# Expert rows added into two rows of DRAM for each token, in place of eight rows written once

## The chip, the cores and the metric

One core of a Trainium2 chip runs the whole kernel in one launch. The metric is the device time of the kernel in microseconds (us). The kernel before takes 988.71 us, the median of three runs (987.71 to 989.04).

## What is computed

One layer of a decoder on 512 tokens of width 1024, in float32. After the mixers and attention comes a mixture of experts, and it is the part that the change touches:

```python
idx, wts = route(h2, w_router[i], router_bias[i])            # 8 of 64 experts for each token
y = swiglu(h_pad[tok], w_gate[e], w_up[e], w_down[e])        # for each expert e, its tokens tok
acc = acc.at[tok].add(y.astype(jnp.float32) * wt[:, None])   # weighted rows, summed for each token
x = x + moe.reshape(B, S, D)                                 # moe: this sum plus a shared expert
ple_gate = jax.nn.sigmoid(rmsnorm(x, g_ple[i]) @ w_ple_gate[i])
x = x + ple_gate * rmsnorm(p[i] @ w_ple_proj[i], g_ple_post[i])
```

So 512 x 8 = 4096 weighted rows of 4 KB each have to be brought together by token. Each expert has three weight matrices of 1 MB, 192 MB in all.

## The kernel before, in words

**Stages.** The dense part (attention, mixers, gates) ends at about 300 us. Then the router, the lists of tokens and the shared expert, then the experts from about 343 us to about 904 us, and then a tail: the sum of the routed rows, and the per-layer gate `w_ple_gate` on the four tiles of 128 tokens.

**The expert loop.** The experts are sorted by the number of their tokens and taken four at a time, in 16 groups. A group is three steps of 128 slots in the first eight groups (96 slots for each expert) and two steps in the others (64 slots each), 40 steps (`STEPS`). No step holds slots of more than two experts. In a step r:

- GpSimd (POOL) gathers 128 token rows from DRAM by an indirect DMA (`gather`, L791), four steps before it handles the output rows of the same step.
- TensorE transposes the rows (L1740), multiplies by the gate and up matrices (`up`, L2196), transposes the activations (L2205) and multiplies by the down matrix (`down(r)`, L2225, one iteration later).
- ScalarE scales the 128 output rows by their weights (`weigh`, L971) into one of two buffers `yrow`.
- GpSimd sends them to DRAM by an indirect DMA (`scatter`, L801 to L810) into `y_dram`, named accumulator in the trace, at row 8 x token + rank, where rank says which of its eight experts this is for the token. Slots with no token have an index out of bounds and move nothing. `scatter(r)` waits for the landing of scatter r-2, which used the same buffer.

SyncE (SP) issues the weight loads in an order written out by hand (`load_group`): each waits until TensorE has finished with its slot of the buffer `ring` (`gu_ps` counts the gate and up products, `y_ps` the down products). After the experts it issues the `w_ple_gate` loads (`load_ple_gate`, L616), which need slots 9, 10, 0 and 11.

**The lists.** Once for all tokens, VectorE (DVE) turns the sorted ranks into a running count over the experts (L1491 to L1499), which becomes the fourth column of `tokw`, beside three bfloat16 parts of the weight. For each group TensorE picks weight and rank of each slot by small matmuls (`lists`), and `weights_of` (L1504 to L1536) turns them into scale and index with seven small VectorE instructions.

**The last group.** Its rows for the first tile of tokens are not scattered; TensorE adds them by `picked_rows` (L2268), and VectorE by `add_picked` (L1617). For this, and for that only, the eight rows of each token of tile 0 were set to zero early on (L502, 4096 KB).

**The tail.** The tokens are cut into ten `PIECES`: four of 256 columns for tile 0, and two of 512 columns for each other tile. `load_rows` (L463) reads eight part rows for each token into the ring: 16 MB in 20 DMAs. `sum_eight` (L1622 to L1624) adds eight to four to two to one, `sum_rows` (L1692) adds the total to x and counts `x2_ready`. TensorE then transposes (`third_T`, L2324), VectorE scales the transposed columns (L1698), and TensorE multiplies by `w_ple_gate` (`ple_gate_part`, L2340). ScalarE takes the sigmoid (L1042), VectorE forms the result (L1711, L1713), SP stores it. Piece 0 is loaded by ScalarE's queue and pieces 1 to 3 by SP before the last scatter has landed, those of tiles 1 to 3 after `experts_done` (set at L847 when all scatters have landed), and the later ones also wait for a buffer: five buffers serve ten pieces (`Y_FREED`).

There is also a path for lists longer than 96 (`further_rounds`); it is not taken with these inputs.

Of the kernel before, what the change touches and what calls it, by code (L numbers as in the profile page):

```python
# [14 lines left out]
P = 128  # L15
# [19 lines left out]
ACC_ROWS = T * TOPK  # L35
# [19 lines left out]
TCOL, WCOL = 2, 4  # L55
# [112 lines left out]
Y_FREED = [0, 0, 0, 0, 0, 1, 3, 4, 5, 6]  # L168
# [11 lines left out]
def build(nc, t, y_dram, h2_dram, out):  # L180
    ctx = ExitStack()
    with ctx:
# [3 lines left out]
        def sem(name):  # L186
# [61 lines left out]
        slot_wr = qa[:, 1024 + 3 * STEPS:1024 + 5 * STEPS].rearrange("p (r c) -> p r c", c=2)  # L248
# [20 lines left out]
        count_of = flat_actT[:, 2 * D:2 * D + 3 * NR].rearrange("p (b i e) -> p b i e", b=2, i=NT)  # L269
# [6 lines left out]
                 for k in range(2)]  # L276
# [6 lines left out]
        pair_sum, pair_own = (small[:, 40 + k * 12:52 + k * 12].rearrange("p (s e c) -> p s e c", e=2, c=2)  # L283
                              for k in range(2))
        ysum = [ring[:, s:s + n // 256, :].rearrange("p u n -> p (u n)").rearrange("p (r n) -> p r n", r=TOPK)
                for s, (_, _, n) in zip(Y_SLOT, PIECES)]

# [63 lines left out]
        y_loaded = [sem(f"y_loaded{b}") for b in range(5)]  # L351
# [82 lines left out]
        y_rows = y_dram.rearrange("(i p r) n -> i p r n", p=P, r=TOPK)  # L434
# [39 lines left out]
        def _(sp):  # L474
# [27 lines left out]
            sp.dma_start(y_rows[0], zero_row.unsqueeze(1).broadcast_to([P, TOPK, D])).then_inc(y_first, 16)  # L502
# [127 lines left out]
            for m in range(2, 4):  # L630
                for c in range(2):
                    load_rows(sp, m, c)

            def o_start(j):
                sp.wait_ge(y_ps, STRIPS * STEPS)
                for b in range(4):
                    sp.wait_ge(y_loaded[b], 32)
# [8 lines left out]
            def o_reload():  # L646
                sp.wait_ge(o_done, 1)
                for m in range(4):
                    for c in range(2):
                        load_rows(sp, m, c, y_first)  # L650
# [16 lines left out]
        def _(pool):  # L667
# [157 lines left out]
            def o_move(e, n, j):  # L825
# [11 lines left out]
                                        yrow[0][0:CAP, :], None, bounds_check=ACC_ROWS - 1, oob_is_err=False  # L837
                                        ).then_inc(o_scattered, 16)
# [21 lines left out]
        def _(act):  # L860
# [104 lines left out]
            def weigh(r):  # L965
                j = r % BUF
                act.wait_ge(y_ps, STRIPS * (r + 1))
                act.wait_ge(list_ready, STEP_OF[r][0] + 1)
                if r >= BUF:
                    act.wait_ge(scattered[j], 16 * (r // BUF))  # L970
                nc.scalar.activation(yrow[j], bank(6, 2), ACT.Copy, scale=slot_wr[:, r, 0:1]).then_inc(y_ready, 1)  # L971
# [21 lines left out]
            for r in range(STEPS):  # L993
# [7 lines left out]
                if r == STEPS - 1:  # L1001
                    for j in range(BUF):
                        act.wait_ge(scattered[j], 16 * len(range(j, STEPS - DIRECT, BUF)))
                    for c in range(2):
                        load_rows(act, 0, c)
# [50 lines left out]
        def _(dve):  # L1056
# [391 lines left out]
            HEAD, SMALL = NE // 2, BIG_GROUPS * GROUP  # L1448
# [38 lines left out]
            nc.vector.tensor_copy(tw3[:, :, 2], rest)  # L1487
# [11 lines left out]
            nc.vector.tensor_scalar(tokw[:, :, :, 3], count_of[:, b, :, HEAD:], -1.0, None, ALU.add  # L1499
                                    ).then_inc(tokw_ready, 1)  # L1500
# [3 lines left out]
            def weights_of(g, found):  # L1504
# [5 lines left out]
                own = cst[:, C_PAIR:C_PAIR + 6] if g < BIG_GROUPS else cst[:, C_PAIR2:C_PAIR2 + 4]  # L1510
                total = pair_sum[:, 0:n, :, :]
                mine = pair_own[:, 0:n, :, :]
                nc.vector.tensor_copy(total[:, :, :, 1], w[:, :, :, 3]).then_inc(dve_step, 1)
                nc.vector.tensor_copy(mine[:, :, :, 0], w[:, :, :, 0]).then_inc(dve_step, 1)
                n_step[0] += 2
                dve.wait_ge(dve_step, n_step[0])
                link(nc.vector.tensor_tensor(total[:, :, :, 0], mine[:, :, :, 0], w[:, :, :, 1], ALU.add))
                link(nc.vector.tensor_tensor(total[:, :, :, 0], total[:, :, :, 0], w[:, :, :, 2], ALU.add))
                link(nc.vector.tensor_tensor(
                    mine, total, own.rearrange("p (s e) -> p s e", e=2).unsqueeze(3).broadcast_to([P, n, 2, 2]),  # L1520
                    ALU.mult))
                link(nc.vector.tensor_tensor(slot_wr[:, r, :], mine[:, :, 0, :], mine[:, :, 1, :], ALU.add))
                rank_of = slot_wr[:, r, 1]
                if g == NGROUP - 1:


                    first, rank_of = small[:, 16:16 + n], small[:, 20:20 + n]
                    link(nc.vector.tensor_scalar(first, row_of[:, r], float(P), float(ACC_ROWS), ALU.is_lt, ALU.mult))
                    link(nc.vector.tensor_tensor(rank_of, first, slot_wr[:, r, 1], ALU.add))
                nc.vector.scalar_tensor_tensor(to_row[:, r], row_of[:, r], float(TOPK), rank_of,  # L1530
# [108 lines left out]
            def o_vector(e, n, j):  # L1639
# [7 lines left out]
                def o_link(ins):  # L1647
# [13 lines left out]
                nc.vector.scalar_tensor_tensor(o_to[0:CAP, :], row, float(TOPK), L[:, 5:6], ALU.mult, ALU.add  # L1661
                                               ).then_inc(o_list_ready, 1)
# [10 lines left out]
            def o_rows():  # L1673
                dve.wait_ge(y_first, 16 * 9)
                nc.vector.tensor_reduce(first_sum, ysum[0].rearrange("p r n -> p n r"), AX_X, ALU.add
                                        ).then_inc(y_first, 1)
                dve.wait_ge(y_first, 16 * 9 + 1)
# [4 lines left out]
            def sum_rows(m):  # L1682
# [3 lines left out]
                total = ysum[m][:, 0, :] if m else first_sum  # L1686
                if m:
                    dve.wait_ge(y_loaded[Y_BUF[m]], 32 * (1 + Y_BUF[0:m].count(Y_BUF[m])))
                    sum_eight(m, total)
# [693 lines left out]
```

## Time and profile before

| | |
|---|---|
| median of 3 runs | 988.71 us (987.71 to 989.04) |
| the profiled execution | 985.47 us |
| span of its profile | 983.6 us |
| mean granted TensorE clock | 0.989 |
| busy: PE, DVE, ACT, POOL | 930.8, 360.6, 162.6, 229.8 us |
| moved by DMA | 298.95 MB |

The profile is of one execution; a sum of its rows is made against its span of 983.6 us, and 985.47 us is that execution's own time, with 1.9 us around the span. Busy time of PE counts overlapping matmuls; shares of DMA are those of the core's 16 DMA engines.

### The profile page before, as it was taken

What the parts mean: (1) busy time and instruction counts of PE and PEld (TensorE: products, weight loads), DVE (VectorE), ACT (ScalarE), POOL (GpSimd) and SP (SyncE); (2) the same over time, 40 slices, a digit from 0 to 9 for tenths busy, and PEclk for the clock granted to TensorE, in tenths of its full rate; (3) what the DMA queues carried; (4) which work ended last, traced back from release to release, by engine and by line L of the source; (5) the groups of instructions that cost most, each with busy time, mean ns of one, the idle gap of its engine ahead of it and who ended that gap; (6) DMA issues with size and microseconds to landing.
All of it is one profiled execution on the core that took longest, in us unless ns stands there. A gap on an engine that the chain in (4) does not pass through costs nothing.

```text
span 983.6 us, 15583 instructions
## 1 busy us (share of the span) xinstructions
PE 930.8 (95%) x6327; PEld 477.3 (49%) x6327; DVE 360.6 (37%) x773; ACT 162.6 (17%) x304; POOL 229.8 (23%) x345
## 2 busy tenths in 40 slices
PE   6999999999999999999999999999879898997698
PEld 4678788888655533333333333333323333332345
DVE  5565673336436743333332111111101111111787
ACT  2001324210011211111111111111101111221021
POOL 4115923162110212222222222211211111101110
PEclk9999999999999999999999999999979999999899
DMA  9930005421393659999999999999999999999972
GB/s 331 332 129 1 1 1 175 167 86 51 131 382 154 214 209 397 398 416 403 406 418 409 409 420 413 419 420 422 412 422 423 419 422 411 420 404 365 379 279 86
DMA packets 81816, 298.95 MB, mean 304 GB/s; under 512 B 9251, under 2 KB 33863, under 8 KB 57552
## 3 DMA queue, kind: packets, MB, share of 16 engines
q1 hardware_dynamic: 68048, 261.09, 67.2%
q0 software_dynamic: 11920, 33.63, 8.7%
q10 hardware_dynamic: 1776, 3.21, 0.9%
q8 instruction: 51, 0.84, 0.3%
q14 instruction: 21, 0.17, 0.1%
HBM read 277.16 MB, written 29.36 MB: 312 GB/s over the span
## 4 chain that ended last, share of the span: by engine, by line
PE 74%; DMA 20%; SPq 3%; DVE 2%; issue 1%; ACT 1%; POOL 0%; POOLq 0%; ACTq 0%
PE ps L2196 23%; DMA ring<-in_w_exp_up 16%; PE ps L1807 12%; PE ps L2225 9%; PE ps L1957 6%; PE ps L1936 5%; PE ps L2340 4%; PE ps L1763 3%; PE ps L1740 2%; SPq L463 2%; PE ps L2012 1%; PE ps L1769 1%; DMA ring<-accumulator 1%; PE ps L2205 1%; DMA accumulator<-actT,stage 1%; SPq L517 1%
## 5 line engine op out<-in xcount | busy, mean ns | idle before, releaser
L2196 PE MATMUL ps<-ring,gates 128*32 128x512 f32 x2560 | 287.7, 601 | 25.4 <-DMA ring<-in_w_exp_up 24.7
L2196 PEld LDWEIGHTS ps<-ring,gates 128*32 128x32 f32 x2560 | 88.0, 111 | 217.3 <-issue 216.4
L2225 PE MATMUL ps<-ring,poolbuf 128*32 128x512 f32 x1280 | 145.6, 595 | 3.1 <-DMA ring<-in_w_exp_down 3.1
L1554 DVE COPY poolbuf<-ps 128x256 f32<-128x256 f32 x40 | 17.0, 425 | 352.7 <-PE ps L2205 352.7
L2225 PEld LDWEIGHTS ps<-ring,poolbuf 128*32 128x32 f32 x1280 | 37.9, 109 | 83.9 <-issue 82.2
L784 POOL COPY stage<-qT 128x1 uint32<-128x1 uint32 x40 | 7.2, 180 | 261.1 <-PE ps L1740 233.4
L971 ACT ACTIVATE actT<-ps,qT 128x1024 f32<-128x1024 f32 x40 | 44.5, 1113 | 142.3 <-PE ps L2225 142.3
L963 ACT ACTIVATE poolbuf<-ps 128x256 f32<-128x256 f32 x40 | 15.3, 384 | 277.5 <-PE ps L2196 277.5
L1807 PE MATMUL ps<-xrow,ring 128*128 128x256 f32 x256 | 57.9, 381 | 0.1
L1957 PE MATMUL ps<-ring,gates 128*128 128x512 f32 x128 | 56.4, 594 | 0.0
L1740 PE MATMUL ps<-cst,rows 128*128 128x128 f32 x352 | 48.5, 285 | 7.8 <-DVE rows L1067 7.7
L773 POOL TENSOR_TENSOR tickets<-cst 128x1 f32<-128x1 f32 x78 | 14.6, 188 | 163.2 <-ACT actT L971 159.8
L1807 PEld LDWEIGHTS ps<-xrow,ring 128*128 128x128 f32 x256 | 48.4, 190 | 8.4 <-issue 1.7
L1740 PEld LDWEIGHTS ps<-cst,rows 128*128 128x128 f32 x352 | 44.7, 193 | 9.9 <-issue 8.5
L1807 PE MATMUL ps<-actT,ring 128*128 128x256 f32 x208 | 47.5, 382 | 0.0
L791 POOL DMA_INDIRECT rows<-h_rows,stage x40 | 42.0, 1050 | 21.0 <-issue 18.8
L808 POOL DMA_INDIRECT accumulator<-actT,stage x40 | 40.6, 1015 | 22.0 <-issue 22.0
L2340 PE MATMUL ps<-ring,actT 128*128 128x512 f32 (+1 forms) x112 | 42.2, 531 | 0.0
L1807 PEld LDWEIGHTS ps<-actT,ring 128*128 128x128 f32 x208 | 39.1, 190 | 6.3 <-issue 0.9
L723 POOL TENSOR_TENSOR ring<-ring 128x1024 f32<-128x1024 f32 x12 | 28.3, 2358 | 52.7 <-DMA ring<-in_w_gate 30.5
L1957 PEld LDWEIGHTS ps<-ring,gates 128*128 128x128 f32 x128 | 23.8, 190 | 26.8 <-issue 26.8
L691 POOL TENSOR_SCALAR st<-st 128x1 f32<-128x1 f32 (+2 forms) x17 | 4.3, 255 | 110.5 <-ACT rows L916 49.7
(288 smaller groups left out, 1069.6 us busy)
## 6 DMA issues: line engine op xcount, KB each, us to landing
ring<-in_w_exp_down SPq DMA_DIRECT2D x64, 1024.0 KB, 17.3
ring<-in_w_exp_gate SPq DMA_DIRECT2D x62, 1024.0 KB, 14.0
ring<-in_w_exp_up SPq DMA_DIRECT2D x62, 1024.0 KB, 15.7
ring<-accumulator SPq DMA_DIRECT2D x12, 1024.0 KB, 13.0
ring<-in_w_gate SPq DMA_DIRECT2D x8, 1024.0 KB, 10.3
ring<-in_w_in SPq DMA_DIRECT2D x5, 1024.0 KB, 12.9
xrow<-in_x SPq DMA_DIRECT2D x8, 512.0 KB, 5.2
accumulator<-ring SPq DMA_DIRECT2D x1, 4096.0 KB, 19.8
```

The source lines that it names most:

```text
L723: nc.gpsimd.tensor_tensor(dst, a, b, ALU.subtract).then_inc(wsum_ready, 1)
L791: pool.indirect_dma_start(hg[j], None, h2_dram, bass.IndirectOffsetOnAxis(ap=stage[:, 0, j, :], axis=0), bounds_check=T - 1, oob_is_err=Fa ...
L808: pool.indirect_dma_start(y_dram, bass.IndirectOffsetOnAxis(ap=stage[:, 1, j, :], axis=0), yrow[j], None, bounds_check=ACC_ROWS - 1, oob_i ...
L971: nc.scalar.activation(yrow[j], bank(6, 2), ACT.Copy, scale=slot_wr[:, r, 0:1]).then_inc(y_ready, 1)
L1740: last = nc.tensor.transpose(bank(b0 + half)[:, k * width:(k + 1) * width], v[0:width, 4 * half + k, :], ident[0:width, 0:width])
L1763: last = mm(bank(2 * (i % 2)), actT[:, k, i * P:(i + 1) * P], qv[:, k], start=(k == 0), stop=(k == KD - 1))
L1807: last = mm(out[:, f * HALF_T:(f + 1) * HALF_T], w[:, k, f * P:(f + 1) * P], x[:, k, :], start=(k == 0), stop=(k == 3))
L1936: last = mm(bank(2 + c % 4)[:, f * HALF_T:(f + 1) * HALF_T], w[:, k, (2 * p + f) * P:(2 * p + f + 1) * P], x[:, k, :], start=(k == 0), sto ...
L1957: last = mm(bank(half), gates[:, k, i * P:(i + 1) * P], w[:, k], start=(n == 0), stop=(n == KD - 1))
L2196: last = mm(bank(2 + k)[part, :], hgT[k][:, q, part], pair_view(EXPERT_SLOT[js[c]])[:, q], start=(q == 0), stop=(q == KD - 1))
L2225: last = mm(bank(6 + half)[part, :], eactT[r % 2][:, q, part], w[:, q, half * 512:(half + 1) * 512], start=(q == 0), stop=(q == 1))
L2340: last = mm(gate_bank(i, n0)[:, 0:width], xT, unit_view(s, 4)[:, k % 4, n0 % 512:n0 % 512 + width], start=(k == 0), stop=(k == KD - 1))
```

## The change

The accumulator shrinks from eight rows for each token to two. A scatter now adds to a row (`compute_op=ALU.add`) in place of writing it. The row is 2 x token + part, where part is 0 or 1 by which of the step's two experts the slot belongs to, so that no DMA names a row twice; since successive DMAs may name the same row, each scatter waits for the landing of the one before it. The 1024 rows are set to zero early by one DMA of 4096 KB, as large as before. The running count, the rank column and part of `weights_of` go. At the end each tile is read by one DMA of 1 MB, tile 0 by ScalarE's queue and the others by SP after `experts_done`; each tile has a ring slot of its own. One addition takes the place of `sum_eight`.

```diff
-ACC_ROWS = T * TOPK
+PARTS = 2
+ACC_ROWS = T * PARTS
...
-Y_SLOT = [1, 3, 4, 7, 5, 1, 3, 7, 5, 1]
-Y_BUF = [0, 1, 2, 3, 4, 0, 1, 3, 4, 0]
+Y_SLOT = [1, 3, 4, 7]
...
-        def load_rows(eng, m, c, done=None):
-            i, c0, width = PIECES[m]
-            eng.dma_start(ysum[m][:, 4 * c:4 * c + 4, :], y_rows[i][:, 4 * c:4 * c + 4, c0:c0 + width]
-                          ).then_inc(y_loaded[Y_BUF[m]] if done is None else done, 16)
+        def load_rows(eng, i, done=None):
+            eng.dma_start(ring[:, Y_SLOT[i], :], y_rows[i]).then_inc(y_loaded[i] if done is None else done, 16)
...
-            sp.dma_start(y_rows[0], zero_row.unsqueeze(1).broadcast_to([P, TOPK, D])).then_inc(y_first, 16)
+            sp.dma_start(y_all, zero_row.unsqueeze(1).broadcast_to([P, ACC_ROWS // P, D])).then_inc(y_first, 16)
...
             load_ple_gate(0, 0)
             load_ple_gate(0, 1)
-            for j in range(BUF):
-                sp.wait_ge(scattered[j], 16 * len(range(j, STEPS - DIRECT, BUF)))
-            sp.wait_ge(gu_ps, STRIPS * STEPS)
-            for c in range(2):
-                load_rows(sp, 1, c)
             load_ple_gate(1, 0)
             sp.wait_ge(y_ps, STRIPS * (STEPS - 1))
             load_ple_gate(1, 1)
-            for m in range(2, 4):
-                for c in range(2):
-                    load_rows(sp, m, c)
...
             sp.wait_ge(experts_done, 1)
-            for m in range(4, NPIECE):
-                if Y_FREED[m]:
-                    sp.wait_ge(x2_ready, Y_FREED[m])
-                load_rows(sp, m, 0)
-                load_rows(sp, m, 1)
+            for i in range(1, NT):
+                load_rows(sp, i)
...
             def scatter(r):
                 j = r % BUF
-                if r >= BUF:
-                    pool.wait_ge(scattered[j], 16 * (r // BUF))
+                if r:
+                    pool.wait_ge(scattered[(r - 1) % BUF], 16 * ((r - 1) // BUF + 1))
...
                 pool.indirect_dma_start(y_dram, bass.IndirectOffsetOnAxis(ap=stage[:, 1, j, :], axis=0),
-                                        yrow[j], None, bounds_check=ACC_ROWS - 1, oob_is_err=False
-                                        ).then_inc(scattered[j], 16)
+                                        yrow[j], None, bounds_check=ACC_ROWS - 1, oob_is_err=False,
+                                        compute_op=ALU.add).then_inc(scattered[j], 16)
...
-                    for c in range(2):
-                        load_rows(act, 0, c)
+                    load_rows(act, 0)
...
-            dve.wait_ge(shared_ps, 2)
-            for b in range(2):
-                nc.vector.memset(count_of[:, b, :, 0:HEAD], 0.0).then_inc(dve_step, 1)
-            n_step[0] += 2
-            link(nc.vector.tensor_scalar(count_of[:, 0, :, HEAD:], rank3, 0.5, None, ALU.is_gt))
-            b, span = 0, 1
-            while span < NE:
-                link(nc.vector.tensor_tensor(count_of[:, 1 - b, :, HEAD:], count_of[:, b, :, HEAD:],
-                                             count_of[:, b, :, HEAD - span:HEAD - span + NE], ALU.add))
-                b, span = 1 - b, 2 * span
...
                 link(nc.vector.tensor_tensor(
-                    mine, total, own.rearrange("p (s e) -> p s e", e=2).unsqueeze(3).broadcast_to([P, n, 2, 2]),
-                    ALU.mult))
-                link(nc.vector.tensor_tensor(slot_wr[:, r, :], mine[:, :, 0, :], mine[:, :, 1, :], ALU.add))
-                rank_of = slot_wr[:, r, 1]
+                    mine, w, own.unsqueeze(3).broadcast_to([P, n, 2, WCOL]), ALU.mult))
+                link(nc.vector.tensor_reduce(slot_w[:, r], mine.rearrange("p s e c -> p s (e c)"), AX_X, ALU.add))
+                part = own[:, :, 1]
...
-            def sum_eight(m, total):
-                y = ysum[m]
-                link(nc.vector.tensor_tensor(y[:, 0:4, :], y[:, 0:4, :], y[:, 4:8, :], ALU.add))
-                link(nc.vector.tensor_tensor(y[:, 0:2, :], y[:, 0:2, :], y[:, 2:4, :], ALU.add))
-                link(nc.vector.tensor_tensor(total, y[:, 0, :], y[:, 1, :], ALU.add))
-            dve.wait_ge(y_loaded[Y_BUF[0]], 32)
-            sum_eight(0, first_sum)
+            def sum_parts(m, total):
+                i, c0, width = PIECES[m]
+                y = ysum[i][:, :, c0:c0 + width]
+                return nc.vector.tensor_tensor(total, y[:, 0, :], y[:, 1, :], ALU.add)
+            dve.wait_ge(y_loaded[0], 16)
+            link(sum_parts(0, first_sum))
```

## Rows read from the trace of the kernel before

**Rows 1.** The page: engine totals, and the span in 40 equal slices.

```profile
PE 930.8 (95%) x6327; PEld 477.3 (49%) x6327; DVE 360.6 (37%) x773; ACT 162.6 (17%) x304; POOL 229.8 (23%) x345
...
PE   6999999999999999999999999999879898997698
...
DMA  9930005421393659999999999999999999999972
GB/s 331 332 129 1 1 1 175 167 86 51 131 382 154 214 209 397 398 416 403 406 418 409 409 420 413 419 420 422 412 422 423 419 422 411 420 404 365 379 279 86
```

**Rows 2.** The page: DMA queues (packets, MB, share of 16 engines' span).

```profile
q1 hardware_dynamic: 68048, 261.09, 67.2%
q0 software_dynamic: 11920, 33.63, 8.7%
```

**Rows 3.** Windows: span, busy of PE, PEld, DVE, ACT, POOL, clock, DMA share, GB/s.

```profile
345.00:380.00 35.00, 34.27 (x360) 13.71 (x355) 13.83 (x46) 5.17 (x8) 6.90 (x15) 1.00 0.70 265
380.00:571.00 191.00, 191.00 (x1920) 73.90 (x1916) 56.88 (x206) 32.39 (x47) 46.93 (x95) 1.00 1.00 409
571.00:630.00 59.00, 58.82 (x534) 21.25 (x526) 6.77 (x15) 10.47 (x15) 14.08 (x30) 1.00 1.01 417
630.00:903.00 273.00, 245.41 (x1850) 90.69 (x1842) 37.67 (x73) 40.47 (x66) 42.07 (x90) 0.97 1.01 415
```

**Rows 4.** Chain that ended last, in order of time (start, length, what): expert stage.

```profile
547.66 6.87 PE ps L2196 x64
...
559.42 6.98 PE ps L2196 x64
...
578.87 15.97 DMA ring<-in_w_exp_up
...
848.10 24.19 DMA ring<-in_w_exp_up
```

**Rows 5.** Timeline of POOL (start, length), one of the 40 steps.

```profile
453.15 1.01 POOL L808 DMA_INDIRECT accumulator<-actT,stage  x1 [0.55 <-issue]
...
460.26 1.04 POOL L791 DMA_INDIRECT rows<-h_rows,stage  x1 [0.50 <-issue]
461.31 0.58 POOL L801 COPY stage<-qT 128x1 uint32<-128x1 uint32 x1
464.55 0.19 POOL L773 TENSOR_TENSOR tickets<-cst 128x1 f32<-128x1 f32 x1 [2.66 <-ACT actT L971]
465.29 1.02 POOL L808 DMA_INDIRECT accumulator<-actT,stage  x1 [0.55 <-issue]
```

**Rows 6.** Chain that ended last: from the last scatters to the end.

```profile
886.53 8.49 DMA accumulator<-actT,stage
...
916.93 11.35 DMA ring<-accumulator
...
940.37 6.87 PE ps L2340 x16
947.23 0.44 PE ps L2324 x4
...
969.61 10.36 PE ps L2340 x40
```

**Rows 7.** Timeline of 868 to 935 us, all engines.

```profile
899.93 3.64 PE L2225 MATMUL ps<-ring,poolbuf 128*32 128x512 f32 x32 [1.02 <-DMA ring<-in_w_exp_down]
...
900.59 0.99 POOL L808 DMA_INDIRECT accumulator<-actT,stage  x1 [0.52 <-issue]
...
903.50 3.70 PE L2268 MATMUL ps<-actT,poolbuf 128*128 128x512 f32 x8
...
905.69 0.99 POOL L808 DMA_INDIRECT accumulator<-actT,stage  x1 [0.53 <-issue]
...
910.95 1.28 DVE L1617 TENSOR_TENSOR xrow<-xrow,ps 128x512 f32<-128x512 f32 x2
912.27 0.43 DVE L1692 TENSOR_TENSOR xrow<-xrow,gates 128x256 f32<-128x256 f32 x1
...
913.25 0.09 POOL L847 MEMSET tickets<- 128x1 f32 x1 [6.56 <-DMA accumulator<-actT,stage]
```

**Rows 8.** Timeline of 335 to 352 us: the running count and what lies beside it.

```profile
343.08 7.07 PE L2196 MATMUL ps<-ring,gates 128*32 128x512 f32 x64
...
344.44 2.73 DVE L1496 TENSOR_TENSOR actT<-actT 128x256 f32<-128x256 f32 x6
```

**Rows 9.** DMA issues: engine, count, KB each, median us to landing.

```profile
ring<-in_w_branch_b SPq DMA_DIRECT2D x2, 1024.0 KB, 5.2
```

More of the change, by code:

```diff
@@ L54 @@
 FIRST_STEP = [STEP_OF.index((g, 0)) for g in range(NGROUP)]
-TCOL, WCOL = 2, 4
+TCOL, WCOL = 2, 3
 LCOL = TCOL + 2 * WCOL
@@ L282, in build @@
         zero_row = ring[:, 10, 0:D]
[L283 to L286, printed above, removed]
+        pair_own = small[:, 40:40 + 3 * 2 * WCOL].rearrange("p (s e c) -> p s e c", e=2, c=WCOL)
+        ysum = [ring[:, s, :].rearrange("p (r n) -> p r n", r=PARTS) for s in Y_SLOT]
         ps = ctx.enter_context(nc.psum_tensor("ps", [P, 8 * 512], F32))
@@ L350, in build @@
         y_first, o_done = sem("y_first"), sem("o_done")
-        y_loaded = [sem(f"y_loaded{b}") for b in range(5)]
+        y_loaded = [sem(f"y_loaded{i}") for i in range(NT)]
         in_first_loaded = sem("in_first_loaded")
@@ L629, in _ @@
             load_ple_gate(1, 1)
-            for m in range(2, 4):
-                for c in range(2):
-                    load_rows(sp, m, c)
             def o_start(j):
                 sp.wait_ge(y_ps, STRIPS * STEPS)
-                for b in range(4):
-                    sp.wait_ge(y_loaded[b], 32)
+                sp.wait_ge(y_loaded[0], 16)
             def o_load(e, n, j):
@@ L647, in o_reload @@
                 sp.wait_ge(o_done, 1)
-                for m in range(4):
-                    for c in range(2):
-                        load_rows(sp, m, c, y_first)
+                load_rows(sp, 0, y_first)
             further_rounds(sp, longest_list(sp), o_start, o_load, o_reload)
@@ L836, in o_move @@
                 pool.indirect_dma_start(y_dram, bass.IndirectOffsetOnAxis(ap=o_to[0:CAP, :], axis=0),
-                                        yrow[0][0:CAP, :], None, bounds_check=ACC_ROWS - 1, oob_is_err=False
-                                        ).then_inc(o_scattered, 16)
+                                        yrow[0][0:CAP, :], None, bounds_check=ACC_ROWS - 1, oob_is_err=False,
+                                        compute_op=ALU.add).then_inc(o_scattered, 16)
                 pool.wait_ge(o_scattered, 16 * (n + 1))
@@ L970, in weigh @@
                     act.wait_ge(scattered[j], 16 * (r // BUF))
-                nc.scalar.activation(yrow[j], bank(6, 2), ACT.Copy, scale=slot_wr[:, r, 0:1]).then_inc(y_ready, 1)
+                nc.scalar.activation(yrow[j], bank(6, 2), ACT.Copy, scale=slot_w[:, r:r + 1]).then_inc(y_ready, 1)
             def ple_square(n):
@@ L1003, in _ @@
                         act.wait_ge(scattered[j], 16 * len(range(j, STEPS - DIRECT, BUF)))
-                    for c in range(2):
-                        load_rows(act, 0, c)
+                    load_rows(act, 0)
                 if r:
@@ L1486, in _ @@
             link(nc.vector.tensor_tensor(rest, rest, tw3[:, :, 1], ALU.subtract))
[L1487 to L1500 removed]
+            nc.vector.tensor_copy(tw3[:, :, 2], rest).then_inc(tokw_ready, 1)
             shared_mult(1)
@@ L1509, in weights_of @@
                 w = found[:, :, TCOL:].rearrange("p s (e c) -> p s e c", e=2)
-                own = cst[:, C_PAIR:C_PAIR + 6] if g < BIG_GROUPS else cst[:, C_PAIR2:C_PAIR2 + 4]
-                total = pair_sum[:, 0:n, :, :]
+                own = (cst[:, C_PAIR:C_PAIR + 6] if g < BIG_GROUPS else cst[:, C_PAIR2:C_PAIR2 + 4]).rearrange(
+                    "p (s e) -> p s e", e=2)
                 mine = pair_own[:, 0:n, :, :]
[L1513 to L1518, printed above, removed]
                 link(nc.vector.tensor_tensor(
-                    mine, total, own.rearrange("p (s e) -> p s e", e=2).unsqueeze(3).broadcast_to([P, n, 2, 2]),
-                    ALU.mult))
-                link(nc.vector.tensor_tensor(slot_wr[:, r, :], mine[:, :, 0, :], mine[:, :, 1, :], ALU.add))
-                rank_of = slot_wr[:, r, 1]
+                    mine, w, own.unsqueeze(3).broadcast_to([P, n, 2, WCOL]), ALU.mult))
+                link(nc.vector.tensor_reduce(slot_w[:, r], mine.rearrange("p s e c -> p s (e c)"), AX_X, ALU.add))
+                part = own[:, :, 1]
                 if g == NGROUP - 1:
-                    first, rank_of = small[:, 16:16 + n], small[:, 20:20 + n]
+                    first, part = small[:, 16:16 + n], small[:, 20:20 + n]
                     link(nc.vector.tensor_scalar(first, row_of[:, r], float(P), float(ACC_ROWS), ALU.is_lt, ALU.mult))
-                    link(nc.vector.tensor_tensor(rank_of, first, slot_wr[:, r, 1], ALU.add))
-                nc.vector.scalar_tensor_tensor(to_row[:, r], row_of[:, r], float(TOPK), rank_of,
+                    link(nc.vector.tensor_tensor(part, first, own[:, :, 1], ALU.add))
+                nc.vector.scalar_tensor_tensor(to_row[:, r], row_of[:, r], float(PARTS), part,
                                                ALU.mult, ALU.add).then_inc(list_ready, 1)
@@ L1660, in o_vector @@
                 nc.vector.tensor_copy(o_from[0:CAP, :], row)
-                nc.vector.scalar_tensor_tensor(o_to[0:CAP, :], row, float(TOPK), L[:, 5:6], ALU.mult, ALU.add
-                                               ).then_inc(o_list_ready, 1)
+                nc.vector.tensor_tensor(o_to[0:CAP, :], row, row, ALU.add).then_inc(o_list_ready, 1)
                 dve.wait_ge(o_hgT_ps, 2 * n + 1)
@@ L1673, in o_rows @@
             def o_rows():
[L1674 to L1677, printed above, removed]
+                dve.wait_ge(y_first, 32)
+                sum_parts(0, first_sum).then_inc(y_first, 1)
+                dve.wait_ge(y_first, 33)
             further_rounds(dve, longest, o_start, o_vector, o_rows)
@@ L1685, in sum_rows @@
                 xs = xrow[:, i, c0:c0 + width]
-                total = ysum[m][:, 0, :] if m else first_sum
+                total = ysum[i][:, 0, c0:c0 + width] if m else first_sum
                 if m:
-                    dve.wait_ge(y_loaded[Y_BUF[m]], 32 * (1 + Y_BUF[0:m].count(Y_BUF[m])))
-                    sum_eight(m, total)
+                    dve.wait_ge(y_loaded[i], 16)
+                    link(sum_parts(m, total))
                 else:
```

9 lines of the change are left out of this document (4 added, 5 removed).

## The prediction

> **What bounds the kernel now.** I read the page first. PE is busy 95% of the span, but the slices show that in the expert stage, from the 16th slice on, the DMA engines are at nine tenths or more too, and that PE has eights and sevens there towards the end while DMA has none until the last two slices [rows 1]. So two resources compete for the title and the share of busy time can't decide it. The windows say which: from 380 to 571 us PE never idles while DMA moves 409 GB/s, and from 571 us on DMA moves 415 to 417 GB/s and PE has gaps, 27.6 us of them from 630 to 903 us alone [rows 3]. The chain of waits agrees: up to 571 us it is PE after PE, a step of 12.1 to 12.2 us each, with a first DMA wait at 578.87 us, and after that it runs along the weight loads [rows 4]. The expert stage is therefore bound by the bytes that the 16 DMA engines move, in its first part by a hair less than PE.
>
> The tail I read from the chain and the timeline together. The last down product starts at 899.93 and ends at 903.57 us. The first x2 piece is ready at 912.70 (912.27 + 0.43), and the chain then runs along the accumulator reads until about 928 us and from 940 us on along PE alone [rows 6, 7]. So the tail has a part that is bound by reading 16 MB and a part that is bound by PE, and I must see how long PE alone would need.
>
> **The price of adding in the scatter.** The software queue moved 33.63 MB in 40 gathers and 40 scatters, so one scatter carries about 0.42 MB (80 DMAs, the same rows in and out). The queues' shares per MB are the same, 0.257% for q1 and 0.259% for q0 [rows 2]: a byte costs the engines the same whoever sends it. Now the accumulating DMA has to read the destination row besides the source row. No row of this trace shows such a DMA, so I bound it. Let e be the extra engine time of a scatter as a multiple of what it takes now. Below, e = 0: the second read hides in the engine. Above, e = 2: read, read and write follow one another where a plain one overlaps read and write. I take e = 1, the nearest row's price per byte applied to a second read of the same length.
>
> The scatters that come while DMA is full and before the last weight lands are r = 1 to 37: the 38th scatter is issued at 886.53, the next at 900.59, after the last weight wait of PE at 899.93 [rows 6, 7]; the first is before 380 us, where the share is 0.70 [rows 3]. That is 37 x 0.42 = 15.5 MB. At 420 GB/s, what the full slices show [rows 1], e = 1 costs 37 us. There is a little room: from 380 to 571 us, 191 x 409/420 = 186, so 5 us of idle engine time take the first of it. **The expert stage grows by 32 us** (e = 0: 0; e = 2: 69).
>
> No run before this one shows a second read's cost; the Trainium skill, "Collectives: The Full Stack", section on the bandwidth ceiling, says that an add in the DMA engine is slowed not by the arithmetic but by two source reads on one ring, at a measured ratio of 1.93 for its ring reduction. By that e would be 0.93 and the growth 29 us, an estimate from that page.
>
> **The new wait.** Scatter r now waits for scatter r-1 before POOL copies its indices. Behind it on POOL stand the ticket, the scatter itself and the next gather. In steady state a scatter is issued at 453.15, the next index copy stands at 461.31, and the next ticket at 464.55, when ScalarE's rows are there [rows 5]. A scatter under full DMA load landed in 8.49 us [rows 6]. So from 453.15 on there are 11.4 us until the rows are ready, and a landing up to 11 us costs nothing. A longer one delays scatters at first without harm, since the buffers `yrow` are needed two steps later and a gather has some two steps of lead. It binds only if landing plus copy, ticket and issue (0.2 + 0.2 + 0.55, about 1.3 us with semaphores) exceeds the step, which will be some 12.8 us when DMA sets it (12.15 x 409/420, and 1.0 us for 0.42 MB at 420 GB/s). From 8.5 us I expect 10 to 11. Priced at nothing in the loop.
>
> **The tail.** What PE has to do from the first x2 piece on: for each tile two halves of 6.87 and 0.44 us [rows 6], 14.6 us, 58.5 us for four tiles (the last one's quarter-width pieces add up to the same). It takes from 912.70 to 969.61 + 10.36 = 979.97, 67.3 us. So 8.8 us are idle for want of rows or for the addition, and these go. The start moves too: tile 0's two rows come in 1 MB instead of 4 MB, before the last products end; then the first x2 piece waits only for the picked rows, 903.50 + 3.70, plus 1.28 and 0.43 [rows 7]: 908.9 instead of 912.7, another 3.8. Together 12.5 us. Against it stands the serial landing of the last two scatters. They are issued at 900.59 and 905.69 now [rows 7]. With the wait the last can't go before 900.6 + 10 + 1.3 = 912, and lands at some 920 (the last one took 7.6 us to the mark at 913.25 [rows 7]); tile 1 is then loaded in about 5 us (a 1 MB load in a quiet stretch landed in 5.2 [rows 9]), added and transposed in 2.5 us: 928. PE is through with tile 0 at 908.9 + 1.2 + 14.6 = 924.7. So 3 us come back. **The tail shrinks by 9 us**, and the reading of 12 MB less is worth no more than that, since PE is what is left.
>
> **The rest, at nothing.** The running count is ten VectorE instructions, six of them 2.73 us together, so at most 4.6 us at that price each, beside TensorE's first products of 7.07 us [rows 8]; its first reader comes at step 1, 12 us later. Without that cover they would be a gain of up to 4.6 us. Four fewer small instructions for each group, two columns fewer in the list matmuls and two additions less for each piece lie on engines that wait for TensorE or DMA in this stage. The zeros are 4096 KB before and after. The `w_ple_gate` loads stand behind every expert weight in SP's queue still, and come earlier than before by the removed waits; they are in time for tile 0 either way.
>
> **Sum.** +32 - 9 = +23 on the profiled span: 983.6 to 1006.6. The profiled execution took 985.47, 3.2 below the median of 988.71; on the median the sum is 1011.7, call it 1012.
>
> **Rivals.** (a) The second read is free or nearly so, e below 0.3. For it: the shares [rows 2] are of packets and not of either direction, so they can't exclude it. Against it: DMA is full, and a read of HBM is what it is full of. The stage grows by 0 to 6 us, the tail gives 9 to 12: 977 to 986, faster. It decides where e falls under about 0.38, where 37e - 5 = 9. (b) e between 0.3 and 0.7: 986 to 1001. (c) Read, read and write don't overlap, or the rows are added with a stall in the engine: e from 1.4 to 2.2, stage +47 to +76, 1027 to 1056. (d) The scatters' own chain becomes the bound: with a landing of 14 us a step of the first eight groups takes 15.3 in place of 12.2, 24 x 3.1 = 74, and the other 16 steps, at 17 us bound by DMA, still take 1 us more each: +90 - 9, 1070. It speaks for it that 8.5 us is already two thirds of a step; against it, that only the engines' part of this landing doubles (6.4 rows of 4 KB for each engine, 1 us at 420/16 GB/s, 2 us when shared with the loads).
>
> **How the numbers follow.** Forecast (e from 0.7 to 1.4) 0.55; (a) 0.13, (b) 0.07, (c) 0.16, (d) 0.09. The time is that of the likeliest, 1012, whose own range is 1001 to 1027. The range for eight in ten leaves out the lower half of (a) and (d) and the end of (c): 983 to 1052. About 0.2%, 2 us, is what a measurement of this kernel can tell from no change. Faster by more than that holds (a) and nothing else, 0.13; within it is the foot of (b), 0.03; slower is the rest, 0.84.
>
> **What would show it.** Right, if in the profile after: the software queue's share of the engines grows by about half of 8.7% or more for the same rows; the steps before 571 us take about 12.8 us in place of 12.15, with DMA and not PE at their head in the chain; the last down product starts near 932 instead of 899.9; POOL's wait for the scatter before shows only small sums; and from the first x2 piece to the end of PE it is about 62 us in place of 67. Wrong, if the last down product stays near 900 (a), if it comes after 950 (c), or if POOL's index copy waits for the landing in every step and PE for ScalarE's or POOL's rows (d). A tail that shrinks by more than 15 us would mean that I missed a wait there.

## The result, and the profile after

The kernel after takes 1022.18 us (median of four runs, 1021.26 to 1023.43) where the kernel before takes 988.21 us (four runs): a ratio of 1.0339 with a 95% interval of 1.0321 to 1.0357, 34 us more. 1012 us was forecast, with a range of 983 to 1052. The direction and the mechanism were right, two terms of the size were not: the expert stage, to the start of the last down product, grew by 47.5 us in place of 32, and the tail shrank by 11.7 in place of 9.

First the page of the profile after: totals, the 40 slices and the queues.

```profile
span 1019.4 us, 15473 instructions
...
PE 943.0 (93%) x6327; PEld 480.5 (47%) x6327; DVE 319.5 (31%) x679; ACT 162.9 (16%) x304; POOL 250.0 (25%) x345
...
DMA  9830005322665489999999999999999999999612
GB/s 331 309 124 1 1 17 191 124 83 83 259 247 227 166 317 390 382 385 358 367 392 344 366 389 349 380 390 402 376 399 396 387 404 386 389 400 353 218 72 83
...
q1 hardware_dynamic: 58976, 248.51, 61.6%
q0 software_dynamic: 11920, 33.64, 12.7%
```

The software queue moves the same 33.6 MB as before [rows 2], but holds the engines for 12.7% of 1019.4 = 129.5 us in place of 8.7% of 983.6 = 85.6. The 43.9 us more are just over the 42.8 that 40 scatters took before (half of 85.6), so e is 1.03 by this view, if the gathers still take their half. The MB listed don't include the second reads; the share does. The same kernel without the add (`e1_plain`, below) lists the same MB at the old share:

```profile
q0 software_dynamic: 11920, 33.63, 8.8%
```

This is why GB/s falls below 400 while DMA stays at nine.

The windows of the same stretches (as in [rows 3]: span, busy of PE, PEld, DVE, ACT, POOL, clock, DMA share, GB/s) show the stage going over to the DMA bound from its first third on:

```profile
380.00:571.00 191.00, 180.03 (x1770) 68.72 (x1763) 47.07 (x148) 29.45 (x43) 48.72 (x85) 0.96 1.00 375
571.00:630.00 59.00, 51.28 (x438) 18.82 (x440) 6.41 (x15) 8.79 (x14) 13.65 (x25) 0.94 0.98 362
630.00:903.00 273.00, 240.33 (x1790) 88.23 (x1786) 35.32 (x68) 38.12 (x61) 54.82 (x96) 0.95 1.01 392
```

Before 571 us PE never waited; now it idles 11 us there, and its granted clock is 0.96 in place of 1.00. The timeline of PE shows how: five waits for gate and up weights up to 630 us, some 40 us apart, of which the three longest are followed by slower products (start, length, and in brackets the idle time and what ended it).

```profile
455.16 9.61 PE L2153 MATMUL ps<-ring,gates 128*32 128x512 f32 x64 [4.50 <-DMA ring<-in_w_exp_up]
...
469.87 7.05 PE L2153 MATMUL ps<-ring,gates 128*32 128x512 f32 x64
...
495.63 7.07 PE L2153 MATMUL ps<-ring,gates 128*32 128x512 f32 x64 [1.31 <-DMA ring<-in_w_exp_up]
537.41 9.44 PE L2153 MATMUL ps<-ring,gates 128*32 128x512 f32 x64 [5.16 <-DMA ring<-in_w_exp_up]
577.39 7.07 PE L2153 MATMUL ps<-ring,gates 128*32 128x512 f32 x64 [1.74 <-DMA ring<-in_w_exp_up]
618.84 9.69 PE L2153 MATMUL ps<-ring,gates 128*32 128x512 f32 x64 [5.98 <-DMA ring<-in_w_exp_up]
```

The slower products run in part at half of the full clock, as this window shows (columns as above, clock 0.50):

```profile
455.10:457.50 2.40, 2.34 (x12) 0.69 (x16) 0.00 (x0) 0.00 (x0) 0.00 (x0) 0.50 1.02 432
```

The waits add up to 18.7 us and the extra length of the three products to 7.6 (9.61 + 9.44 + 9.69 - 3 x 7.05). Scatter 20 is issued at 635.59 us in place of 609.12: 26.5 us later, which is about their sum.

The new wait, in the timeline of POOL one step of the 40, to be read beside [rows 5]:

```profile
440.70 1.61 POOL L789 DMA_INDIRECT accumulator<-actT,stage  x1 [0.55 <-issue]
...
447.81 1.07 POOL L772 DMA_INDIRECT rows<-h_rows,stage  x1 [0.50 <-issue]
451.05 0.18 POOL L782 COPY stage<-qT 128x1 uint32<-128x1 uint32 x1 [2.17 <-DMA accumulator<-actT,stage]
452.10 0.19 POOL L754 TENSOR_TENSOR tickets<-cst 128x1 f32<-128x1 f32 x1 [0.87 <-ACT actT L952]
```

The index copy waits 2.17 us for the scatter before, which landed 10.3 us after its issue, and then POOL still waits 0.87 us for ScalarE's rows. Over the kernel the landings are these (the view of the scatter's line):

```profile
DMA to landing us min/median/max: 4.5/10.5/11.9
```

The tail in the timeline: the last down product, the picked rows, the first x2 piece, the last scatter and the reads.

```profile
947.38 3.64 PE L2182 MATMUL ps<-ring,poolbuf 128*32 128x512 f32 x32 [1.04 <-DMA ring<-in_w_exp_down]
...
950.95 3.70 PE L2225 MATMUL ps<-actT,poolbuf 128*128 128x512 f32 x8
...
953.93 1.45 DVE L1577 TENSOR_TENSOR xrow<-xrow,ps 128x512 f32<-128x512 f32 x2 [5.41 <-PE ps L2225]
955.41 0.42 DVE L1649 TENSOR_TENSOR xrow<-xrow,gates 128x256 f32<-128x256 f32 x1
...
958.90 1.57 POOL L789 DMA_INDIRECT accumulator<-actT,stage  x1 [1.27 <-issue]
```

And its end in the chain that ended last:

```profile
958.90 4.45 DMA accumulator<-actT,stage
...
963.66 4.76 DMA ring<-accumulator
968.42 0.02 issue
968.45 0.70 DVE ring L1583
...
1005.39 10.36 PE ps L2297 x40
```

This chain goes back no further than 957.17 us, so what stands at the head of the early steps is read from the timeline of PE above. From the start of the last down product to the end of the span it is 72.0 us (1019.4 - 947.38); before it was 83.7 [rows 7]. From the first x2 piece, ready at 955.83 (955.41 + 0.42), to the end of PE at 1015.75 it is 59.9 us in place of 67.3.

### The profile page after: what moved, and what is told of

The parts are those of the page before. It is cut to its first block and busy times, and to the rows that moved or that the text cites. A ratio compares the mean times of both kernels' runs of the same rounds, so it can differ in the third digit from the quotient of the medians.

```text
span 1019.4 us, 15473 instructions
## 1 busy us (share of the span) xinstructions
PE 943.0 (93%) x6327; PEld 480.5 (47%) x6327; DVE 319.5 (31%) x679; ACT 162.9 (16%) x304; POOL 250.0 (25%) x345
## 3 DMA queue, kind: packets, MB, share of 16 engines
q0 software_dynamic: 11920, 33.64, 12.7%
## 5 line engine op out<-in xcount | busy, mean ns | idle before, releaser
L2153 PE MATMUL ps<-ring,gates 128*32 128x512 f32 x2560 | 300.2, 623 | 56.5 <-DMA ring<-in_w_exp_up 55.7
L2153 PEld LDWEIGHTS ps<-ring,gates 128*32 128x32 f32 x2560 | 91.3, 114 | 258.5 <-issue 257.6
L789 POOL DMA_INDIRECT accumulator<-actT,stage x40 | 64.2, 1605 | 23.0 <-issue 23.0
L1764 PE MATMUL ps<-actT,ring 128*128 128x256 f32 x208 | 47.5, 381 | 0.0
L1914 PEld LDWEIGHTS ps<-ring,gates 128*128 128x128 f32 x128 | 23.8, 190 | 26.8 <-issue 26.8
## 6 DMA issues: line engine op xcount, KB each, us to landing
ring<-in_w_gate SPq DMA_DIRECT2D x8, 1024.0 KB, 11.7
ring<-in_w_in SPq DMA_DIRECT2D x5, 1024.0 KB, 12.7
```

Of the source, the lines that this page charges most:

```text
L1764: last = mm(out[:, f * HALF_T:(f + 1) * HALF_T], w[:, k, f * P:(f + 1) * P], x[:, k, :], start=(k == 0), stop=(k == 3))
L1914: last = mm(bank(half), gates[:, k, i * P:(i + 1) * P], w[:, k], start=(n == 0), stop=(n == KD - 1))
L2153: last = mm(bank(2 + k)[part, :], hgT[k][:, q, part], pair_view(EXPERT_SLOT[js[c]])[:, q], start=(q == 0), stop=(q == KD - 1))
```

## The experiments

Times are medians beside runs of the kernel before on the same chip (987.5 to 988.3 us in each set); intervals are of the ratio to it.

**Is it the add or the wait?** Three kernels take the change apart. The first takes the add out of the kernel after:

```diff
-                                        yrow[j], None, bounds_check=ACC_ROWS - 1, oob_is_err=False,
-                                        compute_op=ALU.add).then_inc(scattered[j], 16)
+                                        yrow[j], None, bounds_check=ACC_ROWS - 1, oob_is_err=False
+                                        ).then_inc(scattered[j], 16)
```

> The kernel after with a plain writing scatter in place of the adding one; two rows for each token, the wait for the scatter before and the short tail stay (so most expert rows are overwritten and the output lacks them). Theory A (the second read of the adding DMA fills the engines): the expert stage falls back to its old length, the tail stays 11.6 us shorter, about 977 us. Theory B (the wait for the scatter before costs a good part of the 47 us): at least 990 us. Theory C (the tail's gain depends on the shift): not near either.

Measured: 976.09 us, 0.9884 (0.9867 to 0.9900), 11.6 us under the kernel before, and 46.1 under the kernel after. The new wait, with plain scatters, costs about nothing: the last down product starts 1.2 us later than before:

```profile
901.08 3.64 PE L2182 MATMUL ps<-ring,poolbuf 128*32 128x512 f32 x32 [1.79 <-DMA ring<-in_w_exp_down]
```

The tail is 73.3 us long. So nearly the whole growth of the stage goes with the add, and 10.4 us of the tail's gain are there without it.

The second takes the wait away by giving even and odd steps an accumulator each:

```diff
-                if r:
-                    pool.wait_ge(scattered[(r - 1) % BUF], 16 * ((r - 1) // BUF + 1))
+                if r >= BUF:
+                    pool.wait_ge(scattered[j], 16 * (r // BUF))
...
-                pool.indirect_dma_start(y_dram, bass.IndirectOffsetOnAxis(ap=stage[:, 1, j, :], axis=0),
+                pool.indirect_dma_start(y_odd if r % 2 else y_dram,
+                                        bass.IndirectOffsetOnAxis(ap=stage[:, 1, j, :], axis=0),
```

> The kernel after with two accumulators, one for even and one for odd steps, so that a scatter waits for the one before the last only; the tail reads the even one alone (the output lacks the odd steps' rows). The odd one is zeroed by a 4 MB copy while DMA is idle early on. Theory A: same as after, 1020 to 1024 us. Theory B: 1012 us or less.

Measured: 1022.66 us, 1.0360 (1.0343 to 1.0377), as the kernel after. Adds without the wait cost the same.

The third puts the add into the kernel before, into its eight rows, all of which are set to zero early:

```diff
+            for i in range(1, NT):
+                eng.dma_start(y_all[i], y_all[0]).then_inc(y_zeroed, 16)
...
-                                        yrow[j], None, bounds_check=ACC_ROWS - 1, oob_is_err=False
-                                        ).then_inc(scattered[j], 16)
+                                        yrow[j], None, bounds_check=ACC_ROWS - 1, oob_is_err=False,
+                                        compute_op=ALU.add).then_inc(scattered[j], 16)
```

> The kernel before with an adding scatter into its eight rows, all zeroed early while DMA is idle; no new wait, the old tail. Theory A: the expert stage grows by 47 us as in after and the tail keeps its length: 1033 to 1037 us. Theory B (wait): much less of the 47 us, under 1020 us.

Measured: 1034.93 us, 1.0485 (1.0468 to 1.0503): 47.2 us more, with the old wait and the old tail. 47.2 - 11.6 = 35.6 is the change's 34 within the runs' spread. Theory B, the wait, has fallen: the growth is there in both kernels that add without it, and the wait without the add costs 1.2 us.

**Is it the bytes?** The kernel before gets a second transfer behind each scatter. First a plain copy, then half of it:

```diff
+                pool.dma_start(spare[r], h2_dram[0:P, 0:820]).then_inc(y_zeroed, 16)
```

> The kernel before with one plain DMA of 0.42 MB from DRAM to DRAM issued by GpSimd behind each scatter: the same bytes as the second reads, without an add. Theory A (bytes and nothing else): the same growth as the eight-row add, 1033 to 1037 us. Theory D (an add holds the engines longer than its bytes): 10 us or more less, 1025 us at most.

Measured: 1025.93 us, 1.0401 (1.0382 to 1.0420), 38.2 us more; the last down product starts 38.1 us later than before:

```profile
937.99 5.06 PE L2228 MATMUL ps<-ring,poolbuf 128*32 128x512 f32 x32 [2.40 <-DMA ring<-in_w_exp_down]
```

So 0.42 MB cost 0.96 us each over 40 copies, near the 1.0 us of the prediction's price by bytes, but the add costs 9 us more than this. Theory A had 1033 to 1037 us and is missed by 7; theory D had at most 1025 and is missed by 1, so that at this point D stood the better.

> The kernel before with a plain copy of 0.21 MB behind each scatter, half of the extra copy of 0.42 MB that cost 38 us. If bytes cost in proportion, 19 us: 1007 us. If the first 5 us of engine time are free, as the prediction had it, the full copy's 38 was 43 less 5 and the half is 16.5: 1004 us or less.

Measured: 1008.08 us, 1.0211 (1.0193 to 1.0230), 19.7 us more, about half of 38.2. There are no free first 5 us.

Then the same rows a second time, as a plain scatter:

```diff
+                pool.indirect_dma_start(spare, bass.IndirectOffsetOnAxis(ap=stage[:, 1, j, :], axis=0),
+                                        yrow[j], None, bounds_check=ACC_ROWS - 1, oob_is_err=False
+                                        ).then_inc(scattered[j], 16)
```

All waits for a scatter count both.

> The kernel before with every scatter sent twice, as a plain write, the second time into a spare array at the same rows: the same source, the same 4 KB rows, the same 0.42 MB as the second read of an adding scatter. If the adding DMA holds the engines longer than a plain transfer of the same rows, the growth is that of the plain copy, 37 to 40 us: 1025 to 1028 us. If the plain copy was cheap because of its shape (3.3 KB rows, DRAM to DRAM) and rows of a scatter simply cost more, the growth is that of the add, 46 to 49 us: 1034 to 1037 us.

Measured: 1034.38 us, 1.0472 (1.0455 to 1.0490), 46.9 us more, and the last down product where the kernel after has it:

```profile
947.39 3.64 PE L2228 MATMUL ps<-ring,poolbuf 128*32 128x512 f32 x32 [1.24 <-DMA ring<-in_w_exp_down]
```

So the theory that an add holds the engines longer than a plain transfer (D) has fallen too. An adding scatter costs what two plain scatters of the same rows cost; it is rows of these lists that cost a fifth more than the same bytes in an even copy (46.9 against 38.2 us). The copy differs from a scatter in three things, the even spread, the source in DRAM and the rows of 3.3 KB, and this run doesn't tell which of them counts.

**Where in the stage?** The add in one half of the steps only, in the kernel after:

```diff
-                                        compute_op=ALU.add).then_inc(scattered[j], 16)
+                                        **({"compute_op": ALU.add} if r < 20 else {})).then_inc(scattered[j], 16)
```

> The kernel after with the add in the scatters of steps 0 to 19 only, plain writes in the others (so rows are overwritten). Theory A1 (the price is 1.0 to 1.1 us for each adding scatter wherever it stands): 20 us on top of 976, 996 us. Theory A2 (in the first eight groups, where TensorE and DMA are nearly even, an add costs more, because each DMA wait of TensorE is followed by products at half clock): 26 us on top, 1000 to 1004 us. The 5 us of room of the prediction: 991 us.

> The kernel after with the add in the scatters of steps 20 to 39 only, plain writes in the others. Theory A1: 18 to 20 us on top of 976, 994 to 996 us. Theory A2: the same or a little less than A1, 992 to 995 us, and the two halves together give the whole growth of 47 us.

Measured: 1002.60 us, 1.0147 (1.0132 to 1.0163), and 997.63 us, 1.0098 (1.0081 to 1.0114). Against 976.09 without adds that is 26.5 and 21.5 us, 48 together. The second run is the same with `r >= 20`. Theory A1, one price everywhere, missed by 6.6 us on the first half and 1.6 on the second; A2 named the first, but had the second 2.6 us too low.

**Why do listed rows cost more?** A list is cut into strips of 32 slots and fills them from the front; the empty slots move nothing. If a DMA engine serves fixed partitions, the ones that serve the front of a strip carry more rows. Of the 128 slots each engine would have 8. Counted over the lists of this input, with four neighbouring partitions in each 32 of its half of the partitions for an engine, the fullest carries 311 of the 4096 rows and the mean is 256, a factor of 1.21; the double scatter cost 1.23 times the even copy. The Trainium skill, "DMA: Bandwidth & Descriptors", section on the descriptor swizzle, gives that assignment of partitions to engines, for a full 1 MB transfer; no view here shows which engine carries which rows. The test spreads the slots, by one table:

```diff
+    c[:, C_SLOT + 1:C_SLOT + CAP + 1] = slot // STRIP * STRIP + slot % 4 * 8 + slot % STRIP // 4 + 1
...
-                        cst[:, C_IOTA + low:C_IOTA + CAP + 1].unsqueeze(1).unsqueeze(1).broadcast_to(
+                        cst[:, C_SLOT + low:C_SLOT + CAP + 1].unsqueeze(1).unsqueeze(1).broadcast_to(
```

> The kernel before, with one table of constants changed: inside each strip of 32 slots the r-th row of a list goes to slot 4 x (r mod 8) + r div 8 in place of slot r, so that the filled slots of a partly filled strip are spread over the partitions. Same rows, same bytes, same output. Theory E (a list that fills its strips from the front loads some of the 16 DMA engines with more rows than others, and the stage goes by the fullest one: over all steps 311 rows for it against a mean of 256, by counting the lists if each engine serves four neighbouring partitions in each 32 of its half; spread it has 270): gathers and scatters get cheaper, and where DMA sets the pace, from about 571 us on, that shows: 977 to 984 us. If engines don't differ: 987 to 989 us.

Measured: 981.75 us, 0.9941 (0.9928 to 0.9955), 5.8 us less.

> The kernel after with the same table. Theory E: the adding scatter moves three shares of rows in place of two through the fullest engine, so the gain is larger than in the kernel before, 41 rows x 3 x 0.156 us = 19 us at most, nearly all of it where DMA sets the pace: 1003 to 1008 us. If engines don't differ: 1021 to 1023 us.

Measured: 1005.08 us, 1.0180 (1.0160 to 1.0199), 17.1 us less than the kernel after. The windows of this kernel:

```profile
380.00:571.00 191.00, 182.57 (x1826) 71.00 (x1822) 48.41 (x151) 31.41 (x45) 51.85 (x91) 0.99 1.02 389
571.00:630.00 59.00, 58.30 (x530) 21.21 (x525) 6.76 (x15) 9.61 (x15) 15.25 (x28) 1.00 1.02 388
```

The rate listed is 389 GB/s in place of 375, for the same rows and bytes, and PE's clock is back at 0.99 in this stretch. The same permutation gains three times as much where each list passes through the engines three times as where it passes twice and a good part of the stage is bound by PE. Both times lie in the ranges of theory E. Between the two spread kernels the change costs 23.3 us, 36.8 in the stage, near the 38.1 of the even copy; their last down products (the kernel before with the table, then the kernel after with it):

```profile
894.86 3.64 PE L2228 MATMUL ps<-ring,poolbuf 128*32 128x512 f32 x32 [1.05 <-DMA ring<-in_w_exp_down]
...
931.69 3.64 PE L2185 MATMUL ps<-ring,poolbuf 128*32 128x512 f32 x32 [0.94 <-ACT actT L955]
```

The traces hold a second sign. Each landing of a scatter raises its semaphore in 16 steps, as many as there are DMA engines, and the traces keep the time of each step. Over the scatters with all 16 steps kept, the first and the last lie 2.48 us apart on average in the kernel after and 1.44 with the table; in the kernel before it is 1.72 and 1.34. So the table makes the parts of a transfer end closer together. It changes the order of the rows too, and what that does by itself was not tried.

**A version that beats both.** If bytes through the engines are the currency, the rows should be smaller. In the kernel before, the weighted rows are rounded to bfloat16 and the sum is made in float32:

```diff
-        yrow = [flat_actT[:, k * D:(k + 1) * D] for k in range(BUF)]
+        yrow = [flat_actT[:, k * D:k * D + D // 2].bitcast(BF16) for k in range(BUF)]
...
-                link(nc.vector.tensor_tensor(y[:, 0:4, :], y[:, 0:4, :], y[:, 4:8, :], ALU.add))
+                link(nc.vector.tensor_tensor(y, ysum[m][:, 0:4, :], ysum[m][:, 4:8, :], ALU.add))
...
-    acc = nc.dram_tensor("accumulator", (ACC_ROWS, D), F32, kind="Internal").ap()
+    acc = nc.dram_tensor("accumulator", (ACC_ROWS, D), BF16, kind="Internal").ap()
```

> The kernel before, with the weighted rows rounded to bfloat16 by ScalarE and kept so in the eight rows of DRAM, plain writes, summed in float32 at the end; a scatter carries 0.21 MB and the end reads 8 MB. If bytes rule: the first eight groups keep TensorE's pace, the rest gains about 8 to 12 us, the tail another 8 to 12: 964 to 972 us. If 2 KB rows cost as much as 4 KB rows (a price by the row and not by the byte): 980 to 988 us.

Measured over five rounds: 968.40 us, 0.9801 (0.9788 to 0.9815), 20 us less. The last down product of its timeline:

```profile
885.83 3.64 PE L2229 MATMUL ps<-ring,poolbuf 128*32 128x512 f32 x32 [1.02 <-DMA ring<-in_w_exp_down]
```

14.1 us of the gain are in the stage and 3.2 in the tail (80.5 us long), where 8 to 12 had been expected of each: the total came out as forecast, the shares did not. The two make 17.3 us by the profiles and 20 by the medians. It holds the rows at lower precision than the kernel before does.

> The bfloat16 rows of e7 with the same table. Theory E: the gather gains as in e12 and the scatter half as much, in the stretch that DMA bounds: 962 to 966 us. If engines don't differ: 968 us.

Measured: 967.44 us, 0.9794 (0.9778 to 0.9809). This overlaps with the version before it, so the spread table adds nothing that these rounds can tell, and the expectation of 962 to 966 was missed. One reason may be that less is left for DMA to bound: from 571 to 885 us PE waits 15.8 us for weights in the kernel with bfloat16 rows, where it waits 23.8 in the kernel before. But 15.8 us would be room enough for the gain that theory E forecast, and the last down product moved by 1.1 us only (885.83 to 884.74). The 16 steps of a scatter's landing hardly close up either (1.34 us to 1.29). Why the table does so little for these rows is open, and it counts against theory E as it stands.

## Why the prediction was right, and what it sized wrong

- **The bound** was read rightly. The growth comes with the adds, at all places of the stage, and turns the first part from PE to DMA.
- **e = 1** was right as engine time, by two measures: 1.03 by the queue's share, and a second plain scatter in place of the add puts the last down product at the same time (947.39 and 947.38 us). The Trainium skill, "Collectives: The Full Stack", section on the bandwidth ceiling, puts the price down to two source reads, at a ratio of 1.93; here the queue's share gives 2.03, near it. The 29 us that the prediction worked out from it fell as short as its 32.
- **"At 420 GB/s, what the full slices show, e = 1 costs 37 us"** is the term that was mis-sized: the stage grew by 47.5. The price was taken from bytes over the whole core's rate. That is right for a transfer that is spread evenly (38.1 us in the stage for 40 copies), and too low for rows of half-filled lists; that these go at the pace of the fullest engine is the reading that the slot table supports. The queue's share could not show this, since it is a mean over the 16 engines: for copy, double scatter and add it says 12.4%, 12.3% and 12.7%.
- **"There is a little room ... 5 us of idle engine time take the first of it"** was wrong. 409 GB/s beside a DMA share of 1.00 [rows 3] was no idle time: half a copy costs half. Of the 15.5 us by which the stage was missed, 5 are this room, 9.4 the listed rows over the even copy, and 1.1 the copy over 37.
- **Luck** has a part in how near 1022 lies to 1012. By the prediction's own sum, 37 x e - 5, a stage that grows by 47.5 us is e = 1.42, past the forecast's 0.7 to 1.4 and at the foot of rival (c)'s 47 to 76. The time stayed inside the forecast's 1001 to 1027 because the tail gave 2.7 us more than was forecast and the medians differ by 1.8 less than the profiled spans (34.0 and 35.8).
- **The steps before 571 us** were to take 12.8 us; scatters 0 to 22, the last of them behind that stretch, are 13.3 us apart (367.16 to 659.09). The growth comes in jumps of 2 to 9 us and not step by step; the buffers lend PE a few steps of lead, and behind the longer waits the products are slower too. The two lines of [rows 4] lie 11.8 us apart and not 12.1 to 12.2 as the prediction reads them; 12.1 is the mean over the scatters 0 to 20 of the kernel before (367.00 to 609.12).
- **The new wait** at nothing: right. The landing takes 10.5 us where 10 to 11 was expected, and the add costs the same without the wait. The sign that POOL's wait would show only small sums was not met: it is 79.7 us in 25 waits, the four longest (7.2 to 9.6 us) in the last steps. In 22 of the 25 ScalarE's rows come later still, as the line at 452.10 shows, so those waits delay nothing, and rival (d) stays off for that.
- **The tail**: -11.7 measured, -9 predicted. The first x2 piece comes 4.8 us after the last down product's end in place of 9.1 (3.8 gained was forecast, 4.3 measured), and PE has 1.4 us of gaps in place of 8.8. The 3 us that the serial landing was to take back were at most 1.4: with DMA no longer full the last scatter landed in 4.5 us, not 8. The reading of 12 MB less was worth the gaps of PE and the earlier start, and no more.
- **Rivals**: (a) and (b) are excluded by the double scatter and the queue's share. Rival (c) begins at 1027, above the result; its growth of the stage was reached, but its mechanism, reads and write one after the other, would cost more than two plain scatters, and the add costs the same (47.2 and 46.9 us).

Open: why the first 20 steps cost 26.5 us and the last 20 21.5. In the first the trace shows 7.6 us of products at a lower clock behind waits; how much of them the DMA bound would have hidden was not separated. The fullest engine of theory E doesn't explain it, since by the same count it has 156 rows in the first 20 steps and 155 in the last. That single engines are uneven is inferred from the response to the slot table, from the 16 steps of the landings and from the count, not seen; the slot table with bfloat16 rows, which gained next to nothing, is not explained.

## What to carry to other kernels

Here an accumulating scatter cost as much as sending its rows twice. Where the DMA engines are full, adding in the scatter is paid in the loop at full price, while what it saves at the end is only worth the gaps of the engine that remains. Bytes over the core's rate price a scatter of part-filled lists too low, here by a fifth: measure one by sending it twice, and try placing the valid rows evenly over the partitions. A DMA share of 1.00 at a slightly lower rate was no slack.

## What the hardware showed that was not expected

- An adding scatter and two plain ones cost the same to within the runs' spread (47.2 and 46.9 us over 40), while an even copy of the same bytes costs 38.2.
- Permuting slots within strips of 32, with the same rows and bytes, is worth 5.8 us with two passes of each list and 17.1 us with three.
- The issue of an adding scatter holds POOL 1.60 us in place of 1.01; no wait of PE or ScalarE is put down to it.
- After a wait of PE of 4.5 us or more in the first groups, the next 64 products took 9.4 to 9.7 us in place of 7.05, with a mean granted clock of 0.96 from 380 to 571 us and 0.50 from 455.1 to 460 us, just behind the first of these waits; after waits of 1.3 and 1.7 us they took 7.07.
- From the first to the last of the 16 steps of a landing it is 2.48 us for the adding scatter and 1.72 for the plain one, and less in both with the table.
